# A matrix recurrence of 64-row products: four parts of the TensorE array instead of two, and every copy of its chain shared by two engines

## The reference

```python
    def step(S, inp):
        r_t, w_t, k_t, v_t, kk_t, a_t = inp
        sa = jnp.einsum('bhvk,bhk->bhv', S, kk_t)
        S = S * w_t[:, :, None, :] - sa[..., None] * (kk_t * a_t)[:, :, None, :] + v_t[..., None] * k_t[:, :, None, :]
        return S, jnp.einsum('bhvk,bhk->bhv', S, r_t)

    S_out, y = lax.scan(step, S_in.astype(F32), seq)
```

## Time and profile before

| | us |
|---|---|
| median of 3 runs | 1123.25 |
| lowest and highest run | 1123.21, 1129.95 |
| span of the profiled execution | 1120.2 |
| recurrence, prompt tiles, within the span | 547 to 675 |

### The profile page before, as it was taken

One profiled execution on the slowest core, in us unless ns is written; L12 is line 12 of the kernel. 1 busy time (PEld: TensorE's weight loads), 2 busy tenths in 40 slices (PEclk: granted clock), 3 DMA queues, 4 the chain that ended last, 5 costly groups with the idle time before them and its releaser, 6 DMA issues.

```text
span 1120.2 us, 25522 instructions
## 1 busy us (share of the span) xinstructions
PE 1026.5 (92%) x10346; PEld 676.0 (60%) x10346; DVE 497.7 (44%) x1257; ACT 330.4 (29%) x877; POOL 116.9 (10%) x140
## 2 busy tenths in 40 slices
PE   9999997599998499999899999989999948999995
PEld 3687454466664267777788887656555535666641
DVE  1581134322222636497636653866623252222217
ACT  0102114133333233223334332165422132333321
POOL 0010000210000300000211110421000011100013
PEclk9999998699999699999999999899999978999998
DMA  9762204999996631122322233394353089999936
GB/s 317 298 88 65 109 38 194 334 351 373 371 402 251 218 151 60 54 86 75 95 75 77 73 115 99 110 388 183 127 222 150 19 324 285 375 372 378 413 105 222
DMA packets 80861, 225.32 MB, mean 201 GB/s; under 512 B 9424, under 2 KB 50432, under 8 KB 62432
## 3 DMA queue, kind: packets, MB, share of 16 engines
q1 hardware_dynamic: 65184, 153.29, 37.7%
q0 software_dynamic: 11968, 57.71, 15.6%
q10 hardware_dynamic: 3584, 12.58, 3.0%
HBM read 201.57 MB, written 40.86 MB: 216 GB/s over the span
## 4 chain that ended last, share of the span: by engine, by line
PE 86%; DMA 5%; DVE 4%; issue 4%; ACT 1%; POOL 0%; DVEq 0%; POOLq 0%; SPq 0%; ACTq 0%
PE bank L1352 16%; PE bank L1256 10%; PE bank L1543 9%; PE bank L1376 8%; PE bank L1451 6%; PE bank L1642 4%; PE bank L1477 3%; PE bank L1334 2%; PE bank L1514 2%; DMA xkept<-x 1%; PE bank L1896 1%; PE bank L1921 1%; PE bank L1267 1%; DMA work<-xkept,idx 1%; PE bank L1855 1%
## 5 line engine op out<-in xcount | busy, mean ns | idle before, releaser
L1256 PE MATMUL bank<-ring,cat 128*128 128x512 f32 x256 | 112.6, 594 | 1.3 <-ACT cat L2088 1.3
L1543 PE MATMUL bank<-xT,ring 128*128 128x288 f32 x448 | 110.9, 407 | 0.0
L1543 PEld LDWEIGHTS bank<-xT,ring 128*128 128x128 f32 x448 | 84.6, 190 | 23.8 <-issue 1.1
L1352 PE MATMUL bank<-ring,work 128*32 128x128 f32 (+1 forms) x1344 | 82.4, 317 | 1.7 <-DVE work L2537 1.7
L1256 PEld LDWEIGHTS bank<-ring,cat 128*128 128x128 f32 x256 | 47.5, 190 | 57.2 <-issue 57.2
L2547 DVE TENSOR_TENSOR work<-work,bank 128x192 f32<-128x192 f32 x32 | 11.3, 354 | 156.3 <-ACT work L2048 156.3
L2556 DVE COPY work<-bank 64x512 f32<-64x512 f32 x64 | 44.0, 688 | 67.2 <-PE bank L1376 66.7
L1352 PEld LDWEIGHTS bank<-ring,work 128*32 128x32 f32 (+1 forms) x1344 | 57.8, 121 | 24.7 <-issue 12.7
L1451 PE MATMUL bank<-xT,ring 128*128 128x288 f32 x256 | 63.1, 407 | 0.0
L2048 ACT ACTIVATE work<-bank 128x192 f32<-128x192 f32 x32 | 10.6, 331 | 162.3 <-PE bank L1352 162.3
L1451 PEld LDWEIGHTS bank<-xT,ring 128*128 128x128 f32 x256 | 48.3, 190 | 13.5 <-issue 0.4
(11 more groups left out here) (459 smaller groups left out, 1893.8 us busy)
## 6 DMA issues: line engine op xcount, KB each, us to landing
ring<-in_stream_dram SPq DMA_DIRECT2D x61, 1024.0 KB, 9.9
work<-in_stream_dram SPq DMA_DIRECT2D x16, 1024.0 KB, 17.1
cat<-in_stream_dram SPq DMA_DIRECT2D x16, 1024.0 KB, 19.1
by_batch<-in_pages_dram SPq DMA_DIRECT2D x128, 128.0 KB, 2.4
x<-in_stream_dram SPq DMA_DIRECT2D x12, 1024.0 KB, 18.3
xT<-in_stream_dram SPq DMA_DIRECT2D x12, 1024.0 KB, 17.3
yrows<-work ACTq DMA_DIRECT2D x32, 384.0 KB, 7.4
lnp<-in_ln_dram POOLq DMA_DIRECT2D x4, 1024.0 KB, 15.2
```

What stands on the lines that cost most here:

```text
L1256: i = pe.matmul(bank(n)[0:ROWS[tile], :], cat[:, k, tok(tile)], slot(w[k // 4], 4, 512)[:, k % 4, :], start=(k == 0), stop=(k == KC - 1))
L1352: i = pe.matmul(by_half[rows * q:rows * q + rows, :, to:to + width], xgT[:, e % 2, k, at:at + rows], w[:, :, width * q:width * q + width], ...
L1543: i = pe.matmul(bank(n + s)[:, 0:nn], slot(w, KC, 256)[:, k, P * (m % 2):P * (m % 2) + P], xT[:, k, a:a + nn], start=(k == 0), stop=(k == ...
```

## The change

Products of the prompt's recurrence are laid out so that all four parts of the array work. The even half (s = 0) writes a chunk to its own 64 partitions as before, the odd half (s = 1) crosses over: it writes what it read in rows 0 to 63 to partitions 64 to 127 and the other way round (`chunks[k ^ s]`). Both halves of a piece are issued together, in two banks, 16 products in turn. So in the odd half a chunk changes sides with every product of the chain.

The chain is written anew. X is no longer added to: the identity is folded into the weights. GpSimd makes I+M2, I+M4 and I-HT (new semaphore `folded`), VectorE makes I+M8 and I+H2T while it copies, and X1, X2, X3, Z and TT are plain products with these. N4 stands alone instead of NX, H and H2T are new, and Z and TT take the place of Z1, Z2 and TT: 15 chain products in place of 12. M computes eight products more for the odd half, whose Nd is taken from there by a fourth mask, while X0 of the odd half is made from bA. tokV, tokB and tokK become 16 products of 64 columns with an identity.

ScalarE copies the even half of every plain copy of the chain (`BY_BOTH`) and of UW, VectorE the odd half. The order of the list changes with it. EQ and UV keep their order of work and read the crossed layout (`chunks[k ^ s]`), so each of their banks is now written from both row groups, as in the chain, the turned pieces and UW; bA, M and kA keep one bank for each row group. The sample tile keeps its code.

```diff
 PAIRED = ("bA", "M", "kA", "EQ", "UV")
+CHAIN = ("N2", "M2", "N4", "M4", "X1", "M8", "X2", "X3", "Y", "HT", "H", "H2T", "Z", "TT", "G2V")
+TURNED = ("tokV", "tokB", "tokK")
+BY_BOTH = ("N2", "M2", "N4", "M4", "X1", "X2", "X3", "Y", "HT", "H", "Z", "TT", "G2V")
 OFF_PE = ("square", "inv0", "inv1", "inv2", "inv3", "scale", "select")
 
 
@@ -165,12 +168,11 @@
     before = lambda *names: [(name, t - 1, 0) for name in names] if t > 0 else []
     after = lambda *names: halves(t + 1, *names)
     return ((halves(t, "bA", "M", "kA", "N2", "M2") if t == 0 else [])
-            + before("S0") + [("tokV", t, 0), ("tokA", t, 0)] + halves(t, "NX", "M4") + before("S1")
-            + halves(t, "M8", "X2") + before("yS") + halves(t, "X3") + [("tokB", t, 0)] + halves(t, "G2V")
-            + before("mean") + halves(t, "Y") + [("tokK", t, 0)] + before("square") + halves(t, "HT") + after("bA")
-            + halves(t, "Z1") + before("var") + after("M") + halves(t, "Z2") + before("inv0", "inv1") + after("kA")
-            + halves(t, "TT") + before("inv2", "inv3") + after("N2") + halves(t, "UW") + before("scale", "gate")
-            + after("M2") + halves(t, "EQ", "UV"))
+            + halves(t, "tokV") + [("tokA", t, 0)] + before("S0") + halves(t, "N4") + before("yS") + halves(t, "M4")
+            + before("mean", "S1", "square") + halves(t, "X1", "M8") + before("var") + halves(t, "X2")
+            + before("inv0", "inv1") + halves(t, "G2V", "tokK", "X3") + before("inv2", "inv3") + halves(t, "Y")
+            + before("scale", "gate") + halves(t, "tokB", "HT", "H") + after("bA") + halves(t, "H2T") + after("M")
+            + halves(t, "Z", "TT") + after("N2") + halves(t, "UW") + after("kA", "M2") + halves(t, "EQ", "UV"))
...
+                        nd = d["XA" if half == 1 and tile < SAMPLE else "Nd"]
                         landed(pool, rec("bA", tile, half), 1)
-                        pool.tensor_tensor(d["XA"][0:r, half], one, d["Nd"][0:r, half], ALU.subtract).then_inc(x0_ready, 1)
+                        pool.tensor_tensor(d["XA"][0:r, half], one, nd[0:r, half], ALU.subtract).then_inc(x0_ready, 1)
...
+                        landed(pool, rec("M2", tile, 0), 2)
+                        pool.tensor_tensor(d["I+M2"], both, d["M2"], ALU.add).then_inc(folded, 1)
                         if tile > 0:
                             landed(pool, rec("EQ", tile - 1, 0), 2)
                         one = c("ident64").unsqueeze(1).unsqueeze(1).broadcast_to([P, 4, 2, HD])
                         by = dec[:, :, 2 * tile:2 * tile + 2].unsqueeze(3).broadcast_to([P, 4, 2, HD])
                         pool.tensor_tensor(diag, one, by, ALU.mult).then_inc(diag_ready, 1)
+                        landed(pool, rec("M4", tile, 0), 2)
+                        pool.tensor_tensor(d["I+M4"], both, d["M4"], ALU.add).then_inc(folded, 1)
+                        landed(pool, rec("HT", tile, 0), 2)
+                        pool.tensor_tensor(d["I-HT"], both, d["HT"], ALU.subtract).then_inc(folded, 1)
...
+                elif prompt and name == "M":
+                    for s in range(2):
+                        claim(pe, n + s)
+                    for j in range(4):
+                        for s, k in ((0, 0), (1, 1), (0, 1), (1, 0)):
+                            i = pe.matmul(bank(n + s, 2, 4, HD)[chunks[k], 0, j], alpha[rows[s], j, at(k)],
+                                          beta[rows[s], j, at(k)], start=True, stop=True)
+                            if j == 3 and (s, k) == (0, 1):
+                                done(i, n)
+                        for k in (1, 0):
+                            i = pe.matmul(bank(n + 1, 2, 4, HD)[chunks[k], 1, j], beta[rows[1], j, at(k)],
+                                          alpha[rows[1], j, at(k)], start=True, stop=True)
+                    done(i, n + 1)
+                elif prompt and name in CHAIN:
+                    reads = {"N2": ("bA", "M"), "M2": ("bA", "M"), "N4": ("N2", "M2"), "M4": ("N2", "M2"), "X1": ("M2",),
+                             "M8": ("N4", "M4"), "X2": ("X1",), "X3": ("M8", "X2"), "Y": ("X3",), "HT": ("bA", "Y"),
+                             "H": ("bA", "Y"), "H2T": ("HT", "H"), "Z": ("X3",), "TT": ("H2T", "Z"), "G2V": ("kA", "tokV")}
+                    a, b = {"N2": ("Md", "Nd"), "M2": ("Nd", "Md"), "N4": ("M2", "N2"), "M4": ("N2", "M2"),
+                            "X1": ("I+M2", "XA"), "M8": ("N4", "M4"), "X2": ("I+M4", "X1"), "X3": ("I+M8", "X2"),
+                            "Y": ("X3", None), "HT": ("No", "Y"), "H": ("Y", "No"), "H2T": ("H", "HT"),
+                            "Z": ("I-HT", "X3"), "TT": ("I+H2T", "Z"), "G2V": ("G2", "V")}[name]
+                    for other in reads[name]:
+                        landed(pe, rec(other, tile, 0), 2)
+                    if name == "X1":
+                        pe.wait_ge(x0_ready, 2 * tile + 2)
+                    if name in ("X1", "X2", "Z"):
+                        pe.wait_ge(folded, 3 * tile + 1 + ("X1", "X2", "Z").index(name))
+                    for s in range(2):
+                        claim(pe, n + s)
+                    for j in range(4):
+                        for s in range(2):
+                            for k in range(2):
+                                moving = c("ident64")[chunks[k], :] if b is None else d[b][chunks[k], s, j, :]
+                                i = pe.matmul(bank(n + s, 4, HD)[chunks[k ^ s], j], d[a][chunks[k], s, j, :], moving,
+                                              start=True, stop=True)
+                            if j == 3:
+                                done(i, n + s)
+                elif prompt and name == "UW":
+                    landed(pe, rec("tokA", tile), 1)
+                    for other in ("G2V", "TT"):
+                        landed(pe, rec(other, tile, 0), 2)
+                    for s in range(2):
+                        claim(pe, n + s)
+                    for j in range(4):
+                        for s in range(2):
+                            for k in range(2):
+                                i = pe.matmul(bank(n + s, 4, 2, HD)[chunks[k ^ s], j], d["TT"][chunks[k], s, j, :],
+                                              AG[chunks[k], :, s, j, :], start=True, stop=True)
+                            if j == 3:
+                                done(i, n + s)
...
+                elif prompt and name in TURNED:
+                    if name != "tokV":
+                        pe.wait_ge(decayed, 2 * tile + (1 if name == "tokB" else 2))
+                    src = {"tokV": V_, "tokB": beta, "tokK": kappa}[name]
+                    for s in range(2):
+                        claim(pe, n + s)
+                    for j in range(4):
+                        for s, k in four:
+                            i = pe.matmul(bank(n + s, 4, HD)[chunks[k ^ s], j], src[rows[s], j, at(k)],
+                                          c("ident64")[rows[s], :], start=True, stop=True)
+                            if j == 3 and k == 1:
+                                done(i, n + s)
...
-                if name == "NX":
+                if prompt and name in CHAIN:
+                    if name in BY_BOTH and half == 0:
+                        take(act, n)
+                        give(act.copy(d["GV" if name == "G2V" else name][:, half], bank(n, 4, HD)), n)
+                elif prompt and name in TURNED:
                     take(act, n)
-                    act.copy(d["N4"][0:r, half], bank(n, 4, 2, HD)[0:r, :, 0]).then_inc(n4_copied, 1)
-                elif name in ("N2", "M2", "M4", "M8", "Y", "HT", "G2V"):
+                    give(act.activation(d[name[3]][:, half], bank(n, 4, HD), ACT.Copy, scale=(-1.0 if name == "tokB" else 1.0)), n)
+                elif prompt and name == "UW":
+                    if half == 0:
+                        take(act, n)
+                        give(act.copy(WU[:, :, half].rearrange("p w j v -> p j w v"), bank(n, 4, 2, HD)), n)
...
-                        dve.tensor_tensor(d["Nd"][0:r, half], by_alpha, mask("Nd"), ALU.mult)
+                        nd = d["XA" if half == 1 and prompt else "Nd"]
+                        dve.tensor_tensor(nd[0:r, half], by_alpha, mask("Nd"), ALU.mult)
                         if prompt:
...
+                    i = dve.tensor_tensor(d["Md"][0:r, half], src, mask("Md"), ALU.mult)
+                    if half == 1 and prompt:
+                        i = dve.tensor_tensor(d["Nd"][:, half], bank(n, 2, 4, HD)[:, 1], mask("Nd"), ALU.mult)
+                    give(i, n)
+                elif prompt and name in CHAIN:
+                    if name in ("M8", "H2T"):
+                        take(dve, n)
+                        one = c("ident64").unsqueeze(1).broadcast_to([P, 4, HD])
+                        give(dve.tensor_tensor(d["I+" + name][:, half], src, one, ALU.add), n)
+                    elif name in BY_BOTH and half == 1:
+                        take(dve, n)
```

(18 more changed lines are left out.)

177 lines of the change are left out of this document (90 added, 87 removed).

## The result

The changed kernel takes 1128.9 us (median of 14 runs, 1125.9 to 1132.7) against 1123.2 for the kernel before, run beside it (14 runs, 1119.3 to 1131.0): a ratio of 1.0043, 95% interval 1.0026 to 1.0061. It is 0.4% slower, clear of 1 but within the 1% that I called no change, and 14 us above the forecast of 1115.0. A second measurement of the same program, among the experiments, gave 1129.4.

The account below looks back on a forecast made before the run. TensorE was taken to bound prompt tiles before the change, the chain's waits after it. Gains of 3.4 + 4.0 + 2.5 = 9.9 us, less 1.7 for the clock, took 1123.25 to 1115.0, own range 1109 to 1121.

Parts of the forecast that it names:

- The walk: One prompt tile timed through its waits: ends at 29.2 us, 22.0 of products and 7.2 of idling, against 31.2 before.
- rival D: VectorE copies from PSUM slower than additions, 0.45 against 0.33 us, 4 us in all: 1119; in the forecast's 0.50.
- What four parts are worth: Prompt tile's steps: 16 products of 64 columns on four parts of the array taken at 0.50 us, from M's 29 ns.
- TensorE after, 22.0: TensorE's products in one prompt tile sum to 22.0 us after the change, 28.3 before.
- term for the clock: One fall of TensorE's clock to its lower level for 3.5 us at an idle stretch before TT, costing 1.7 us.
- Tile 3's gain: Last prompt tile, 31.6 us: 2.5 gained, with three masks less (-1.0) and single-part sample products on its tail (+0.5).
- Rival B: Clock falls in two idle stretches of each tile, before bA and TT: 13.6 us against 9.9, 1127; chance 0.15.
- A: Tile period 26 to 28 us by better overlap, 1104.6 at 27, chance 0.20; TensorE-bound end case about 1090, 0.05.
- C: Four parts don't run together when both row groups write one bank: 26.8 us more in all, 1140; chance 0.10.

Follow-up runs that it names:

- e2_burst: Changed kernel with 504 more products of H in tile 1 alone, nothing to wait for between them: 1158.3 us in its one run.
- e3_fewer: Changed kernel with tokV, tokB, tokK, H and G2V at 8 products instead of 16, half the results left out: 1130.7 us, ratio 1.0085.
- e1: Changed kernel with the products of H issued four times, 48 more in each prompt tile: 1139.3 us, ratio 1.0145.
- e4: Changed kernel with the prompt tiles' four norm reciprocals over 16 columns instead of 128: 1122.1 us, ratio 0.9987.
- e6: Changed kernel with reciprocals over 16 columns, and tokV, tokB, tokK, H and G2V as 8 products of 128 columns: 1122.8 us, ratio 0.998.
- e9: Changed kernel with the prompt tiles' norm as exp(-0.5 ln(x + eps)) on ScalarE, without VectorE's four reciprocals: 1127.0 us, ratio 1.0022.
- e12: Changed kernel with short reciprocals, five steps as 8 products of 128 columns and a filling product before TT's wait: 1121.0 us, ratio 0.9951.
- e19: Changed kernel with the norm taken out of VectorE's dense run and five steps as 8 products of 128 columns: 1123.8 us, ratio 0.9988.
- e15_late_tall: Changed kernel with the norm out of VectorE's run; tokV, tokB, tokK at 12 products, four of them 128 columns wide: 1149.3 us, ratio 1.0233.
- e16_after: The changed kernel itself run once more, with no edit: 1129.4 us.
- e10: Changed kernel with short reciprocals and one filling product of 128 rows by 512 columns before TT's wait: 1124.3 us, ratio 0.9995.
- e11: Changed kernel with five steps as 8 products of 128 columns and a filling product before TT, VectorE's work whole: 1126.5 us, ratio 1.0016.

## Why the prediction was wrong

**Right: where the change acts.** The walk's waits are there. VectorE's run (inv0 to gate's end 7.2, forecast 7.35), the order of copies and the price of a copy (rival D is wrong) stand in the rows above. So do the three waits, but shorter than forecast in tile 2: 0.66 before Y (1.6), 0.86 before bA (1.85), 1.95 before TT (2.6). That the idle time of a middle tile came out right in sum, 7.2 forecast and 7.3 measured, is luck, since 2.9 of the 7.3 are stalls that the forecast didn't have. So is the verdict of the same within 1%: I had it as a gain of 0.7%, and it is a loss of 0.4%.

**Wrong: the step "What four parts are worth".** I took the 29 ns of M's 16 products and gave it to every step of the tile, with nothing in the sum for the supply of instructions. For single steps it holds: at 623.78 and 624.29 two of them start 0.51 us apart. But M's 16 products are a quarter of a block. The rate over a block is 58 to 62 ns, as e2_burst shows, because the next 256 instructions come 3.7 to 4.0 us after the last. At 58 ns a product the fetch just fits, so the kernel before, which ran its chain on two parts, never showed it: the trace of before has no stall inside a step. The change made each product cheaper in the array, where time was not to be had for long, and added 44 of them, 176 instructions a tile, where it was.

**Wrong: the term "TensorE after, 22.0".** It is 24.9 in tile 2. Part of it is that a step followed by an idle stretch pays its own drain: a row of the chain says 0.69, and I counted 0.50 for dense work. Its timeline has nine idle stretches in tile 2, each with some 0.2 of drain before it: 1.8 of the 2.9 us (an estimate from these two numbers). Another 0.6 is tokB, whose last records come late: it takes 1.17 us from start to start in tile 2, where it takes 0.52 in tile 1, again 1.3 us behind the landing of a packet. The rest I can't assign.

**Wrong by place: the walk.** Against its marks, tile 2 has inv0 at 11.1 instead of 10.05, gate's end at 18.4 (17.4), UW at 25.7 (24.2) and UV's end at 32.4 (29.2). 1.1 is lost before inv0 (a stall of 0.76 lies there), 0.5 between gate and UW, and 1.8 from UW to UV's end (1.28 of it the stall before EQ). So two stalls, 2.0 us, are most of the 3.2 by which the tile is longer than forecast, and the others lie under VectorE's run. Tile 0 tells it best, since it has no work on a tile before it: forecast 24.6, measured 28.0, stalls 3.6. Without its term for the clock I had the four tiles 9.9 us shorter, and they are 2.6 longer: 12.5 us, beside stalls of 13.2. That the two are so near is in part chance. The stalls are not all on the path: e3_fewer took a third of them away, and waits took their place. Tile 3's gain has a slip of its own: 29.2 - 1.0 + 0.5 is 28.7, which against 31.6 is 2.9 and not 2.5.

**The clock.** The forecast's one fall (1.7) did not come in the profile of after, and two came in the second one (637 and 668), with the end of UV within 1 us of each other: too small a term to see. Rival B is wrong as a forecast of this kernel, and its 1127 near by luck, though e1, e3, e4, e6 and e9 show its mechanism, with two or three falls each beside the one at the recurrence's start.

**Rivals.** A supposed that TensorE would bind at 22 to 27: wrong. C had the right rate, 58 ns a product, and the wrong cause: the parts do run together, bank shared or not (64 products in 2.1 us in e2_burst), so what the prediction cites of the Trainium skill, page TensorEngine Tiling (Array Packing), section Gotcha 1: PSUM Pressure, is not seen here for different rows of a bank. What I left out is a rival in which the supply of instructions, not an engine, becomes the bound.

**What stays open.** The medians differ by 5.7 us, the recurrence by 2.6 in the traces. The other 3 belong to what lies behind UV of tile 3, where the work is the same and single executions scatter by 9 us with the granted clock. The changed kernel's 14 runs had a mean granted clock of 0.954, those of the kernel before beside the experiments 0.957. Why it is lower is not shown, and differences of 3 us between medians of kernels here can come from it alone. How the loss divides between the supply and VectorE's order isn't shown either. Whether a tile could get below 29 us with instructions and VectorE both eased and the clock held was tried only in pieces (e12, e19). No version with all of the work beat the kernel before.

## What to carry to other kernels

When a change makes TensorE's instructions shorter rather than fewer, count instructions as well as time: here a block of 256 needs 3.7 to 4.0 us (e2_burst), so float32 products of 64 columns cannot run under 60 ns for long, whatever part of the array they use. Take a rate from a run of several hundred instructions, not from a burst of sixteen. Read a gap marked issue in the middle of a step as a want of instructions, look whether it ends behind a packet of the instruction queue (1.2 to 1.6 us here), and give work back in wider products (128 columns to an instruction) before giving it more parts of the array.

## What the runs showed of the hardware

- TensorE's instructions come in packets of 256, one in 3.7 to 4.0 us in a stream that waits for nothing else (e2_burst), and the next starts only 0.5 to 1.2 us before the last is used up: a semaphore wait does not let it get ahead (after: packets at 635.60 and 640.35 around the wait before TT).
- A step of eight products of 64 x 64 with four of 64 x 128 among them takes 2.77 us, where 16 of 64 x 64 take 0.5 to 0.7 (e15_late_tall).
- An idle stretch of 1.7 to 2.6 us was followed by a clock of 0.50 for 3.4 us in many traces and not in others with the same waits (after: 1.95 before TT, no fall; e16_after: the same 1.95, a fall). With a product of 128 x 512 in that wait there was none behind it (e10, e11, e12).
- Behind the recurrence the same work took 450 to 453 us in executions with the granted clock at 0.50 for 54 us or more of it, and 444 to 448 in those with 48 or less.
- A table load of ScalarE is 1.28 us, and the two functions of e9_lnexp, used in turn, pay it each time.
